# Block masks added inside the sparse attention, norm weights from three rows, separate statistics for queries and keys

## The reference

```python
proj = h @ w_in
q, kc, vc, ks, vs, kw, vw, gates = jnp.split(proj, split_pts, axis=-1)
q = rms_norm(q.reshape(B, S, G, HPG, DK), q_norm)          # 16 heads of 64
k_cmp = rms_norm(compress_blocks(to_kv(kc), ...), k_norm_cmp)
v_cmp = compress_blocks(to_kv(vc), ...)
o_cmp, p_cmp = compressed_attention(q, k_cmp, v_cmp, pos, slopes)
sel = select_blocks(p_cmp, S)      # imp = sum of p_cmp over a group's heads, top 8 of 16 blocks of 64 keys
o_slc = selected_attention(q, rms_norm(to_kv(ks), k_norm_slc), to_kv(vs), pos, sel, slopes)
o_win = window_attention(q, rms_norm(to_kv(kw), k_norm_win), to_kv(vw), pos, slopes)
o = g[0] * o_cmp + g[1] * o_slc + g[2] * o_win             # g = sigmoid(gates)
```

## Time and profile before

| | us |
|---|---|
| median of 3 runs | 2379.27 (2377.95 to 2382.49) |
| profiled execution | 2378.9 |
| its span, first to last instruction | 2377.1 |
| busy: PE, DVE, ACT, POOL | 2119.5, 960.4, 717.8, 474.0 |
| input projection of layer 1 | 1088 to 1329 of the span |
| compressed attention | 1329 to 1416 |
| sparse attention | 1416 to 1807 |

### The profile page before, as it was taken

The page is one execution under the profiler, slowest core; times in us unless marked ns, Lnnn a source line. Parts: engine busy times, 40 slices in busy tenths (PEclk is TensorE's granted clock), DMA queues, the critical chain, the costliest instruction groups (busy, mean ns, idle before and its releaser), DMA issues. The chain is left out here.

```text
span 2377.1 us, 32726 instructions
## 1 busy us (share of the span) xinstructions
PE 2119.5 (89%) x12669; PEld 1469.5 (62%) x12669; DVE 960.4 (40%) x2286; ACT 717.8 (30%) x1775; POOL 474.0 (20%) x617
## 2 busy tenths in 40 slices
PE   6997759999899999967999648999999999999995
PEld 3444336655688888843654525666665568888883
DVE  3997864532512111113123576666662242111111
ACT  3014455511111111130121656676662111111110
POOL 0001003321112222100000334454441001222211
PEclk9998769999899999989999779999999998999998
DMA  5000011031779999954000100001002147999995
GB/s 204 0 0 0 0 62 37 19 101 71 298 270 358 366 368 368 325 171 106 0 1 0 74 1 10 11 20 45 10 10 74 62 173 275 360 366 370 369 349 137
DMA packets 88034, 347.27 MB, mean 146 GB/s; under 512 B 16721, under 2 KB 21864, under 8 KB 70919
## 3 DMA queue, kind: packets, MB, share of 16 engines
q1 hardware_dynamic: 69446, 278.03, 30.4%
q0 software_dynamic: 18432, 67.12, 10.9%
HBM read 288.84 MB, written 60.47 MB: 147 GB/s over the span
## 5 line engine op out<-in xcount | busy, mean ns | idle before, releaser
L1530 PEld LDWEIGHTS experts_gu_ps<-experts_x_cols,moew_gate 128*128 128x128 f32 x2048 | 242.3, 195 | 34.3 <-issue 34.3
L1530 PE MATMUL experts_gu_ps<-experts_x_cols,moew_gate 128*128 128x128 f32 x2048 | 243.2, 278 | 4.6 <-DVE experts_x_cols L1567 4.6
L1530 PE MATMUL experts_gu_ps<-experts_x_cols,moew_up 128*128 128x128 f32 x2048 | 239.1, 275 | 0.0
L1530 PEld LDWEIGHTS experts_gu_ps<-experts_x_cols,moew_up 128*128 128x128 f32 x2048 | 233.8, 192 | 0.0
L1541 PE MATMUL experts_y_ps<-moew_down,experts_hid 128*128 128x512 f32 x512 | 230.5, 593 | 2.0 <-DVE trunk_x_rows L1623 2.0
L1070 POOL TENSOR_SCALAR nsaatt_probs<-nsaatt_probs,nsaatt_inv,trunk_gates_or_logits 128x384 f32<-128x384 f32 (+7 forms) x256 | 181.6, 726 | 209.3 <-DVE nsaatt_inv L1095 209.3
L1616 DVE TENSOR_TENSOR experts_sig<-experts_gu_ps,experts_sig 128x256 f32<-128x256 f32 x64 | 27.2, 425 | 440.3 <-ACT experts_sig L1579 440.3
L1041 ACT ACTIVATE nsaatt_probs<-nsaatt_probs,nsaatt_bias 128x384 f32<-128x384 f32 (+7 forms) x256 | 169.0, 667 | 17.7 <-DVE nsaatt_bias L1090 17.7
L1470 POOL DMA_INDIRECT x_kept<-trunk_x_rows,moe_index x64 | 101.4, 1585 | 308.0 <-DVE trunk_x_rows L1623 214.0
L1541 PEld LDWEIGHTS experts_y_ps<-moew_down,experts_hid 128*128 128x128 f32 x512 | 92.5, 191 | 95.4 <-issue 95.4
L1579 ACT ACTIVATE experts_sig<-experts_gu_ps 128x256 f32<-128x256 f32 x64 | 24.7, 386 | 416.6 <-PE experts_gu_ps L1530 416.6
(11 more groups left out here) (377 smaller groups left out, 3229.1 us busy)
## 6 DMA issues: line engine op xcount, KB each, us to landing
moew_gate<-in_moe_w_gate_dram SPq DMA_DIRECT2D x64, 1024.0 KB, 7.5
moew_up<-in_moe_w_up_dram SPq DMA_DIRECT2D x64, 1024.0 KB, 11.8
moew_down<-in_moe_w_down_dram SPq DMA_DIRECT2D x64, 1024.0 KB, 15.1
trunk_x_rows<-in_x_dram SPq DMA_DIRECT2D x16, 512.0 KB, 4.7
x_kept<-trunk_x_rows SPq DMA_DIRECT2D x16, 512.0 KB, 2.6
h_rows<-out_h_rows SPq DMA_DIRECT2D x16, 512.0 KB, 2.6
trunk_x_rows<-x_kept SPq DMA_DIRECT2D x16, 512.0 KB, 4.1
l0b_w_in<-in_mix_w_in_dram SPq DMA_DIRECT2D x1, 5760.0 KB, 23.7
```

The costliest lines, as they stand in the source:

```text
L1530: last = pe.matmul(to, wm[:, c, half * P:(half + 1) * P], x_cols[:, s % 2, c, :], start=(c == 0), stop=(c == CHUNKS - 1))
```

## The change

Five edits, all in layer 1:

- The gains come as three rows (`head_gain`), loaded by SP ahead of `second_norm`. The per-head products of the query gain read the one row, and stand behind the reads of the compression's PSUM (`scale_gain`). The key products take the gain through a repeated view.
- Squares, sum, root and scaling are done for the 16 query heads and the four key heads apart (`PARTS`), each with its own semaphore counts; PE transposes the query groups as soon as their rows are ready.
- The compression's last transpose moves from tile 7 to tile 6, and DVE's copy of it behind tile 6.
- `choose` ends with the 16 numbers per row and tile, kept in `left_out`. The eight adds per group go into `attend` (`prepare`, `choose_blocks`): one ahead of the first mask of each step of the group's first pair.
- The adds of the last pair into `p_sum` go from POOL to DVE (`add_last`).

```diff
 def mask(s, i):                                          # attend, DVE
     dve.wait_ge(scored, BR * s + r + 1)
     if s >= BUFS and i == 0:
         dve.wait_ge(turned, first[s - BUFS + 1])
+    if prepare and i == 0:
+        prepare(dve, s, prepared)
     dve.tensor_tensor_reduce(part(s, r, h), scores_of(s, r, h), br["mask"], 1.0, -3e38, ALU.add, ALU.max,
...
 def nsa_inputs(...):
-            @block.sync
-            def _(sp):
-                for h in range(NSA_HEADS):
-                    sp.dma_start(gain[:, h, :], A["nsa_q_norm"][0].partition_broadcast(P)).then_inc(here, 16)
...
                 def columns(t):                          # PE
-                    pe.wait_ge(rows_ready, 3 * (t + 1))
+                    pe.wait_ge(rows_ready, 3 * t + 1)
                     for g in range(GR):
+                        if g == GR - 1:
+                            pe.wait_ge(rows_ready, 3 * (t + 1))
...
-                    if t == 7:
+                    if t == 6:
                         compress_turn()
...
+                def take_squares(t, part):               # ACT
+                    if t:
+                        act.wait_ge(reduced, 2 * (t - 1) + part + 1)
+                    act.activation(square[:, PARTS[part], :], rows[:, t % 2, PARTS[part], :], ACT.Square).then_inc(squared, 1)
...
                     take_queries(t)                      # now ends with take_squares(t, 0)
                     if t:
                         columns(t - 1)
+                    root(t, 0)
                     take_keys_and_gates(t)               # now with take_squares(t, 1)
-                    root(t)
+                    root(t, 1)
...
+                def scale_gain():                        # DVE
+                    dve.wait_ge(head_gain_here, 16 * 3)
+                    for h in range(NSA_HEADS):
+                        dve.tensor_scalar(gain[:, h, :], head_gain[:, 0, :], HD ** -0.5 / SLOPES[h], None, ALU.mult).then_inc(gain_ready, 1)
+
+                def normalise(t, part):
+                    b, heads = t % 2, PARTS[part]
+                    n = heads.stop - heads.start
+                    dve.wait_ge(squared, 2 * t + part + 1)
+                    if t:
+                        dve.wait_ge(rstd_ready, 2 * (t - 1) + part + 1)
+                    dve.tensor_reduce(total[:, heads], square[:, heads, :], X_AXIS, ALU.add).then_inc(reduced, 1)
+                    dve.wait_ge(reduced, 2 * t + part + 1)
+                    mine.link(dve.tensor_scalar(total[:, heads], total[:, heads], 1.0 / HD, RMS_EPS, ALU.mult, ALU.add))
+                    mine.link(dve.reciprocal(total[:, heads], total[:, heads]))
+                    dve.wait_ge(rstd_ready, 2 * t + part + 1)
+                    dve.tensor_tensor(rows[:, b, heads], rows[:, b, heads], over(rstd[:, b, heads].unsqueeze(2), (P, n, HD)),
+                                      ALU.mult).then_inc(scaled, 1)
+                    dve.wait_ge(scaled, 2 * t + part + 1)
...
 def compressed(...):                                     # POOL, DVE
+                    if i == PAIRS - 1:
+                        break
                     pool.wait_ge(p_ready, i + 1)
...
+                def add_last():
+                    i = PAIRS - 1
+                    total_of = p_sum[:, i // PER_GROUP_PAIRS, :, 1:W + 1]
+                    dve.wait_ge(p_ready, i + 1)
+                    for h in range(2):
+                        dve.wait_ge(added, 2 * i + h)
+                        dve.tensor_tensor(total_of, total_of, p[:, i % 2, :, h, 0:W], ALU.add).then_inc(added, 1)
...
-                    to = chosen if g == 0 else near
-                    for t in range(TILES):
-                        at, n = causal_at(t), (t + 1) * P // SLC_BLOCK
-                        dve.tensor_tensor(to[:, at:at + n * SLC_BLOCK].rearrange("p (j k) -> p j k", j=n),
...
 def nsa_attention(...):
+    def choose_blocks(dve, s, prepared):
+        pair, i = divmod(s, TILES)
+        g, first_pair = divmod(pair * KV_GROUPS, PAIRS)
+        if first_pair:
+            return
+        t = TILE_ORDER[i]
+        at, n = causal_at(t), (t + 1) * P // SLC_BLOCK
+        dve.tensor_tensor(chosen[g][:, at:at + n * SLC_BLOCK].rearrange("p (j k) -> p j k", j=n),
+                          near[:, at:at + n * SLC_BLOCK].rearrange("p (j k) -> p j k", j=n),
+                          over(left_out[:, g, t, 0:n].unsqueeze(2), (P, n, SLC_BLOCK)), ALU.add).then_inc(prepared, 1)
+        dve.wait_ge(prepared, g * TILES + i + 1)
...
 def layer1(...):
+            for i, norm in enumerate(("nsa_q_norm", "nsa_k_norm_slc", "nsa_k_norm_win")):
+                nc.sync.dma_start(head_gain[:, i, :], A[norm][0].partition_broadcast(P)).then_inc(head_gain_here, 16)
             second_norm(...)
...
+            nc.vector.wait_ge(near_here, 16)
```

More of the change, by code:

```diff
@@ L2318, in hide, with compressed @@
         pool.engine_nop().then_inc(self.pool_done, 1)
-def compressed(nc, q_cols, k_cmp_pair, v_cmp_pair, near_cmp, seen_cmp, fixed, free, slopes, small_here, near_here, gates, near, chosen,
-               o_all, ident):
+def compressed(nc, q_cols, k_cmp_pair, v_cmp_pair, near_cmp, seen_cmp, fixed, free, slopes, small_here, gates, left_out, o_all, ident):
     W = N_CMP
```

87 lines of the change are left out of this document (37 added, 50 removed).

## The result

The changed kernel takes 2359.61 us (median of four runs, 2359.12 to 2362.08); the kernel before took 2378.73 us beside it on the same chip. The ratio is 0.9917 with a 95% interval of 0.9905 to 0.993: the kernel is faster by 0.7 to 0.95%. The forecast was 2357.9 us, 1.7 us under the measured median, and the range 2350 to 2367 holds it.

A forecast was written before the change was run, and what follows sets the result against it. PE fills the projection loop, so only its ends and DVE's chains in the compressed attention give time. The terms sum to -21.4 us: 2378.9 - 21.4 + 0.4 = 2357.9 us, with 8 in 10 for 2350 to 2367.

The forecast's parts named there:

- What bounds: Projections: PE is full inside the loop, so only its two ends count; compressed attention: the chain runs through DVE.
- 1. First wait: Start of the projections: PE's 11.36 us wait and 2.25 us of low clock go; -13.6 us, bounds -11.4 to -13.6.
- 2. Three broadcasts: Start of layer 1's norm: x comes late behind SP's issues and the queued broadcasts; +2.3 us, range +1.3 to +4.3.
- Nothing hides it: Layer 1's norm: x's delay is paid, as ACT's norm chain and SP's later issues start there, ahead of the next stage.
- 3. Separate statistics: End of the projections: only the keys are left; PE covers the loop's added work; -6.7 us, bounds -5.5 to -7.2.
- 4 and 5. Selections and last pair: Compressed attention: eight adds leave each selection, -5.4 us twice; DVE adds the last pair, -1.4, bounds 0 to -3.0.
- 6. Sixteen adds: Sparse attention: block adds ahead of the masks lengthen PE's waits; +9.3 us, bounds +3.0 to +15.
- Rival D: Sparse attention: DVE and POOL lock each other at the 16 adds, up to 32 us, ending at 2380.6; chance 0.03.
- 7. Clock: Starts of the two attention stages: PE enters after shorter idle times; -0.5 us.
- A (adds hidden): Sparse attention: the block adds are hidden because DVE waits for PE; +3 to +5, about 2352 us; chance 0.15.

The follow-up runs named there:

- e8: The kernel before with only DVE's reads of the compression PSUM put ahead of the sixteen gain products: 2366.2 us, ratio 0.9937.
- a2: The changed kernel once more, nothing altered, to see how far stages vary from profile to profile: 2360.72 us, ratio 0.9918.
- e5: The changed kernel with queries' and keys' statistics taken together again: 2368.11 us, ratio 0.9944.
- e4: The changed kernel with the sixteen block adds back at the end of the two selections: 2362.52 us, ratio 0.9925.
- e6: The changed kernel with the last pair's sum added by POOL again: 2362.69 us, ratio 0.9921.
- e1: The changed kernel with each of the sixteen block adds issued ahead of DVE's wait for the scores: 2353.26 us, ratio 0.9888.
- e7: The changed kernel with e1's edit and the three broadcasts issued by SP inside the input projections: 2349.63 us, ratio 0.9872.
- e9: As e7, with the last two small compression loads also issued behind the border into the projections: 2348.61 us, ratio 0.9865.

## Why the prediction was right, point by point

*What bounds.* Right: with PE full in the loop only the two ends of the projections and the DVE chains outside them gave time.

*1. First wait, forecast -13.6.* Right: -13.38 with 0.33 us of transposes moved in, -13.77 in e8, where nothing else differs. The clock's part (9.28 to 7.03 us) came too.

*2. Three broadcasts, forecast +2.3.* The mechanism was right, the term too small: +3.96 and +4.23 (a2). The step that failed is the choice between the two rates of the earlier trace rows: I took the one with mixed sources (2.2 us), "since the three have three sources", and the delay at ACT's first square came to 4.7 us (1.4 of SP's issue and 3.3 in the queue), a little over what the row with a single source gives (4.3) and over my range at that square. Three sources did not help: from 1047.5 to 1050.5 us, while hardly anything but the broadcasts moves, 195 packets pass in 3 us, fewer than the 90 per us of the single-source row. Nor was "Nothing hides it" quite right: of the 4.7 us 0.7 was won back in SP's later issues (most of it in the first compression weights, 16.46 us instead of 17.39), which is why the stage stayed within the range. The stage's end hangs on SP: its issues of x are held back by the queue, and the projections start 0.5 us behind SP's last issue. The Trainium skill's rule (DMA: Bandwidth & Descriptors, "Two DMAs through the same engine are not ordered"), that descriptors in one queue start in order, agrees: the delay is 6.88 us with the broadcasts ahead of x and 3.58 us with them behind it.

*3. Separate statistics, forecast -6.7.* Right, -7.13: 5.87 are theirs, 0.67 the finer wait ahead of the queries' transposes, 0.59 the compression's end at tile 6. The loop hid the added instructions (body 215.17 in e5 too).

*4 and 5. Selections and last pair, forecast -12.2, with the clock at most -12.7.* Right: -12.51. e4 gives 11.0 for the two selections (forecast 10.8), e6 gives 1.2 for the last pair (forecast 1.4). DVE's wait behind POOL's product was priced correctly from the one collision in the earlier trace rows: the first add ends 0.54 us behind the product, where the forecast had 0.6.

*6. Sixteen adds, forecast +9.3.* Right: +9.94, or 9.6 over all kernels. At the start of the second group's adds the period of eight steps grew by 3.9 us (forecast 4.1). PE's waits for the masks grew by 3.8 us in the first half and 3.1 in the second, those for DVE's copies by 1.1 and 1.3. The collisions with POOL cost DVE little: the longest excess was 0.36 us (a 128-wide add of 0.65 us in group 2 against 0.29 in group 1), where a POOL product was already running. Where DVE came first, POOL paid. The widest case, DVE and then POOL:

```profile
1403.95 1.12 DVE L2536 TENSOR_TENSOR l1c_chosen<-l1c_near,l1c_left_out 128x896 f32<-128x896 f32 x1 [1.74 <-PE nsaatt_scores L990]
...
1404.11 1.50 POOL L1071 TENSOR_SCALAR nsaatt_probs<-nsaatt_probs,nsaatt_inv,trunk_gates_or_logits 128x384 f32<-128x384 f32 x1
```

The same product takes 0.67 us a pair later, with no add beside it. The rule of the Trainium skill (SBUF — State Buffer, "SBUF: two separate sides") that the forecast named, a lock held for the whole instruction by whichever came first, agrees with both: the add keeps its length, and the product ends 0.54 us behind it. Rival D needed 1.9 us per add; 0.6 was paid.

*7. Clock, forecast -0.5.* Small and about right: the first scores of the compressed attention take 7.22 us instead of 7.46, with PE idle for 0.94 us ahead of them both times.

The sum over the changed stretches is -19.1 against -21.4 forecast. Of the 2.3 us missing, 1.7 are part 2 and 0.6 part 6. Untouched code gave another -0.6 between these two profiles; over all profiles its stretches vary by some 3 us, which is why the small terms are judged by stretch and not by the kernel's time; that the forecast lies within 1.7 us of the median is in part luck. Of the rivals, A (adds hidden) was false where the change put them and true one line higher, where e1 moved them.

## What to carry to other kernels

Work that an engine does for its next wait belongs ahead of that wait: the same sixteen adds cost 9.6 us behind the wait for the scores and about 0.5 us ahead of it, and the sign to look for is idle time in the bracket of the added instruction itself. A small transfer is priced by what is queued behind it, on the issuing engine and in the DMA queue, not by its bytes; at a border that all engines cross, look at which engine's last instruction ends just ahead of the next stage, since here it was SP's list of issues (moving its last two small ones behind the border shortened the stage by 1.5 us, e7 to e9).

## What the runs showed of the hardware that was not expected

- Transfers of 128 packets of 256 bytes are quick if each reads its own row (landed in 1.9 us, x behind them 0.1 us late) and slow if all read one row (3.2 us, x 1.7 us late); from the small norm tensors at that place slower still (3.9 to 6.1 us, x 3.3 us late), for a reason left open.
- One broadcast of 768 bytes per partition delays what follows as much as three of 256 (5.34 and 5.30 us from x's issue to its first square): fewer packets of the same bytes bought little but SP's issue time (0.95 of 1.15 us).
- SP's issue of a transfer stretches when the queue ahead is slow: four issues of x took 5.42 us behind the broadcasts and 3.19 us without them.
- When a DVE add of two SBUF inputs and a POOL product overlap, the later one pays: a 128-wide add took 0.65 us instead of 0.29 behind a running product, and a product took 1.50 us instead of 0.67 behind a running 896-wide add.
